# A hybrid retention / gated-attention / mixture-of-experts step on one core: 112 slots per expert block instead of 104, four modulation chunks moved into the second attention's tile loop, three waits moved

## The reference

```
mod = silu(c) @ w_ada + b_ada                       # 6 rows of 1024 for each of 9 conditions
h   = rms_norm(x, norm_pre_mix) * (1 + sc1) + sh1
mix = retention heads (4 x 128) and gated-linear-attention heads (4 x 64 -> 128), then @ w_out
x   = x + g1 * rms_norm(mix, norm_post_mix)
h   = rms_norm(x, norm_pre_ffn) * (1 + sc2) + sh2
f   = shared SwiGLU(h) + sum over 8 of 64 experts of weight * SwiGLU_e(h)   # FF = 256
x   = x + g2 * rms_norm(f, norm_post_ffn)
```

## Time and profile before

| | before |
|---|---|
| median of 3 runs | 1509.92 us (1502.13 to 1510.57) |
| the profiled execution | 1510.28 us |
| its span | 1508.4 us (1.9 us lie around it) |
| PE / DVE / ACT / POOL busy | 1290.0 / 875.9 / 600.8 / 220.2 us |
| moved by DMA | 339.20 MB |

### The profile page before, as it was taken

How to read it: one execution, slowest core, us unless ns; L and a number is a source line. 1 busy time by engine, 2 the same in 40 slices (tenths; PEclk the granted TensorE clock), 3 DMA queues, 4 the chain that set the end, 5 groups by cost and what they waited for, 6 DMA issues and landing times.

```text
span 1508.4 us, 18589 instructions
## 1 busy us (share of the span) xinstructions
PE 1290.0 (86%) x5990; PEld 856.4 (57%) x5990; DVE 875.9 (58%) x1354; ACT 600.8 (40%) x711; POOL 220.2 (15%) x184
## 2 busy tenths in 40 slices
PE   8899999697887896849759999999999999999810
PEld 1599999551455133344446766666666666666500
DVE  0621341243322823246548888888788777788777
ACT  1332221102203001110227767676766666666501
POOL 0100000000000200010012232222222223232211
PEclk9699999897855798959869999999999999999955
DMA  8232221407300591120399999999999999999796
GB/s 330 80 115 91 65 65 33 115 7 237 120 1 4 160 273 50 49 84 1 127 332 357 366 369 365 367 364 365 365 374 357 366 359 355 361 357 372 293 321 223
DMA packets 93567, 339.20 MB, mean 225 GB/s; under 512 B 14360, under 2 KB 37928, under 8 KB 67468
## 3 DMA queue, kind: packets, MB, share of 16 engines
q1 hardware_dynamic: 75104, 301.01, 57.2%
q0 software_dynamic: 18432, 37.79, 7.5%
HBM read 315.13 MB, written 40.39 MB: 236 GB/s over the span
## 4 chain that ended last, share of the span: by engine, by line
PE 52%; DMA 32%; DVE 8%; ACT 3%; issue 3%; SPq 1%; POOL 0%; POOLq 0%; DVEq 0%; ACTq 0%
DMA expert_rows<-arena,row_idx 14%; PE ps L1556 12%; DMA arena<-in_w_exp_down 12%; PE ps L1761 5%; PE ps L1892 4%; PE ps L1587 3%; DMA arena<-expert_rows 2%; PE ps L1797 2%; PE ps L1876 2%; PE ps L1872 2%; PE ps L1504 2%; PE ps L1873 2%; PE ps L1874 2%; DVE down_lo L1398 2%; ACT down_hi L971 2%
## 5 line engine op out<-in xcount | busy, mean ns | idle before, releaser
L1403 DVE TENSOR_TENSOR gu_lo<-w_gu,gu_hi 128x1536 fp32r<-128x1536 f32 x128 | 224.4, 1754 | 2.9 <-ACT gu_hi L965 1.4
L1398 DVE TENSOR_TENSOR down_lo<-arena,down_hi 128x2048 fp32r<-128x2048 f32 x64 | 146.7, 2292 | 85.1 <-ACT down_hi L971 85.1
L965 ACT ACTIVATE gu_hi<-w_gu 128x1536 fp32r<-128x1536 f32 x128 | 189.5, 1481 | 0.1
L1872 PE MATMUL ps<-gu_hi,xT_hi 128*104 128x512 f32 x384 | 157.7, 411 | 12.0 <-issue 7.0
L737 POOL DMA_INDIRECT expert_rows<-arena,row_idx x64 | 104.4, 1631 | 428.2 <-DMA expert_rows<-arena,row_idx 197.2
L1873 PE MATMUL ps<-gu_lo,xT_hi 128*104 128x512 f32 x384 | 153.0, 398 | 0.0
L1874 PE MATMUL ps<-gu_hi,xT_lo 128*104 128x512 f32 x384 | 152.5, 397 | 0.0
L1556 PE MATMUL ps<-w_hi,hT_hi 128*128 128x300 f32 (+1 forms) x480 | 145.8, 304 | 2.3 <-DVE w_lo L1037 2.3
L1556 PE MATMUL ps<-w_lo,hT_hi 128*128 128x300 f32 (+1 forms) x480 | 145.3, 303 | 0.0
L1556 PE MATMUL ps<-w_hi,hT_lo 128*128 128x300 f32 (+1 forms) x480 | 145.1, 302 | 0.0
L971 ACT ACTIVATE down_hi<-arena 128x2048 fp32r<-128x2048 f32 x64 | 122.4, 1912 | 55.4 <-DMA arena<-in_w_exp_down 55.2
(11 more groups left out here) (267 smaller groups left out, 1957.6 us busy)
## 6 DMA issues: line engine op xcount, KB each, us to landing
w_gu<-in_w_exp_gate SPq DMA_DIRECT2D x64, 1024.0 KB
w_gu<-in_w_exp_up SPq DMA_DIRECT2D x64, 1024.0 KB
arena<-in_w_exp_down SPq DMA_DIRECT2D x64, 1024.0 KB
arena<-in_w_ada SPq DMA_DIRECT2D x24, 1024.0 KB, 5.5
arena<-in_w_in SPq DMA_DIRECT2D x12, 1200.0 KB, 5.7
arena<-expert_rows SPq DMA_DIRECT2D x9, 1024.0 KB, 15.9
arena<-expert_rows SPq DMA_DIRECT2D x4, 2048.0 KB, 14.6
arena<-in_x_prompt SPq DMA_DIRECT2D x8, 512.0 KB, 10.5
```

What stands on the lines that cost most here:

```text
L965: a.activation(gu_hi[b % RING][:, :, ks], w_gu[b % U][:, :, ks], ACT.Copy).then_inc(s_ghi, 1)
L1398: v.tensor_tensor(down_lo[:, :, :], w_dn[b % RING], down_hi[:, :, :].bitcast(F32), ALU.subtract).then_inc(s_dlo, 1)
L1403: v.tensor_tensor(gu_lo[b % U][:, :, ks], w_gu[b % U][:, :, ks], gu_hi[b % RING][:, :, ks].bitcast(F32), ALU.subtract).then_inc(s_glo, 1)
L1872: pe.matmul(out, x_hi, gu_hi[r][:, :, k], start=(k == 0), stop=False)
```

## The change

- `T` goes from 104 to 112 (with it the sizes of the slot buffers and the bound `MAX_BLOCKS`, from 108 to 105).
- PE and DVE wait for the states where head 0 first uses them, and not ahead of the retention.
- The store of the prompt state counts on `s_st`. DVE no longer waits for the stores ahead of the gate copies; it waits for the states and the prompt store ahead of the log gates.
- Chunks 0 to 3 of the second modulation leave their two places. `mod_part` issues a quarter of a chunk (two of the eight matmuls; the last with the bias), and tile t of the tile loop, t = 0 to 3, holds the four parts of chunk t; all four use PSUM bank 2. `mod_fold(t - 1)` stands at the head of DVE's tile t.

```
-T = 104
+T = 112
-        MOD2_BANK = (4, 5, 6, 2, 2, 3, 6, 7)
+        MOD2_BANK = (2, 2, 2, 2, 2, 3, 6, 7)
...
-            sp.dma_start(ret_p[0, 0].rearrange("h d v -> d h v"), ret_out).then_inc(s_out, 16)
+            sp.dma_start(ret_p[0, 0].rearrange("h d v -> d h v"), ret_out).then_inc(s_st, 16)
...
@@ vector
-            v.wait_ge(s_st, 16 * (1 + H))
             for h in range(H):
...
                 v.wait_ge(s_rso, h + 1)
+                if h == 0:
+                    v.wait_ge(s_st, 16 * (1 + H))
...
             v.wait_ge(s_rste, 1)
-            v.wait_ge(s_out, 32)
...
+            v.wait_ge(s_st, 16 * (2 + H))
             v.wait_ge(s_l, 2)
...
-            for n in range(3):
-                mod_fold(n)
...
-            mod_fold(3)
             for t in range(NT):
                 R = ROWS[t]
+                if t:
+                    mod_fold(t - 1)
...
@@ tensor
+            def mod_part(n, part):
+
+                i, ks = 2 * n + part // 2, (0, 1) if part % 2 == 0 else (2, 3)
+                if part % 2 == 0:
+                    pe.wait_ge(s_wada[i % 3], 16 * (i // 3 + 3))
+                for k in ks:
+                    o = pe.matmul(ps[0:NCOND, MOD2_BANK[n]], condT[:, 4 * (part // 2) + k, :], w_mod2[i % 3][:, k],
+                                  start=(part == 0 and k == 0), stop=False)
+                if part % 2:
+                    o.then_inc(s_ada, 1)
+                if part == 3:
+                    pe.wait_ge(s_rows, 16 * 6)
+                    pe.matmul(ps[0:NCOND, MOD2_BANK[n]], K("ones", 33)[32:33, 0:NCOND], mod2_bias[:, n], start=False, stop=True).then_inc(s_mod, 1)
...
-            pe.wait_ge(s_st, 16 * (1 + H))
             for h in range(H):
...
                 if h:
                     pe.wait_ge(s_rsoe, h)
+                if h == 0:
+                    pe.wait_ge(s_st, 16 * (1 + H))
...
-            for n in range(3):
-                mod_mm(n)
             pe.wait_ge(s_ls, 2)
...
-                    mod_mm(3)
-                    pe.wait_ge(s_fold, 2 + 3)
...
+                if t < PT:
+                    pe.wait_ge(s_fold, 2 + t)
+                    mod_part(t, 0)
                 pe.wait_ge(s_gte, 2 * t + 2)
...
                         o.then_inc(s_kv, 1)
+                        mod_part(t, 1 + c)
+                    mod_part(t, 3)
                 pe.wait_ge(s_gp, t + 1)
```

More of the change, by code:

```diff
@@ L375, in hybrid_step @@
         s_pj_ev = sem("proj_ready")
-        s_st = sem("states_in")
+        s_st = sem("states_in_and_prompt_state_out")
         s_v = sem("vector_step")
@@ L580, in _ @@
             sp.wait_ge(s_goe, NT)
-            sp.wait_ge(s_out, 16 * (2 + 2 * H))
+            sp.wait_ge(s_out, 16 * (1 + 2 * H))
             sp.dma_start(w_out_buf, w_out[0].rearrange("(k p) n -> p k n", p=P)).then_inc(s_wout, 16)
@@ L685, in _ @@
                 sp.dma_start(tok_rows(y_prompt, y_sample, t), ranks_high[t][0:ROWS[t], 1]).then_inc(s_out, 16)
-            sp.wait_ge(s_out, 16 * (2 + 2 * H + NT))
+            sp.wait_ge(s_out, 16 * (1 + 2 * H + NT))
         @block.gpsimd
@@ L1579, in _ @@
                         project(2 * i + b, b, t)
-            def mod_mm(n):
[L1583 to L1591, removed]
+            def mod_part(n, part):
[10 more added lines that the diff above has]
+                    pe.matmul(ps[0:NCOND, MOD2_BANK[n]], K("ones", 33)[32:33, 0:NCOND], mod2_bias[:, n], start=False, stop=True).then_inc(s_mod, 1)
+            def mod_mm(n):
+                for part in range(4):
+                    mod_part(n, part)
             pe.wait_ge(s_const, 32)
```

## The result

The changed kernel takes 1456.47 us (median of 4 runs, 1451.47 to 1460.36) against 1508.43 us of the kernel before: ratio 0.966, with a 95% interval of 0.9616 to 0.9705. The direction held. The range (1455 to 1494) held by 1.5 us, and only because I had drawn it out to a rival to which I gave 18 in 100; the forecast's own range, 1466 to 1486, did not hold. I forecast 35 us less and it is 52. The two profiled executions are further apart than the medians, 1510.3 to 1451.5 us, of which 4.5 us arose ahead of any edit: the retention's operands are ready at 276.4 us before and at 271.9 after. In the twelve profiles of the changed kernel and its variants, whose code is alike up to there, that point lies between 271.9 and 276.7 us.

What follows compares the result with a forecast made beforehand. Bounds: transfer waits and PE's order before the tile loop, PE at 1.2 GHz in it, serial scatters in the expert blocks. 1510.3 - 8.0 (states) - 9.4 (stores) - 23.4 + 4 + 1.3 + 3 - 2 (chunks) + 0 (slots) = 1475.8, called 1475; range 1455 to 1494.

Steps and rivals of the forecast that it cites:

- a rival to which I gave 18 in 100: Expert blocks: 112 rows shorten the scatter until PE is the bound, 18 us less, result 1458; chance 18 in 100.
- The dealing: Expert blocks' gathers and scatters: each transfer uses the most DMA engines, up to 16, dividing its rows (13 at 104, 16 at 112).

## What to carry over

Where an indirect transfer shares busy DMA engines with other loads, count its packets and try row counts that give fewer of them: 112 or 105 here, not 104 and least of all 108. It is one number, and it was worth 21 us, two thirds as much as the careful edits of the order together. When one row of a profile contradicts a rule, look for the form of the rule that the row fits before setting it aside. Work that is moved into a gap should end just where the next busy stretch begins, since that stretch then starts at the high clock (here that was worth 1.6 us). A shared semaphore that counts loads nobody needs yet is a wait of its own.

## What was unexpected in the hardware

- Packets of an indirect transfer follow the divisors of its rows: 144, 128, 160, 128 with 104, 105, 108, 112 rows. 105 rows cost less than 104, and 108 most.
- The number of slots shows in other transfers: ACT waited 55.2 us for the down weights with 104 slots, 21.3 with 105, 37.9 with 108 and 0 with 112, and the 1 MB reads behind the blocks landed in 15.9 us against 12.6 to 13.1 with 112. The dealing alone does not explain it: with 104 slots and both transfers at 112 rows these are 51.5 and 15.1 us.
- Mixed sizes (gather 104, scatter 112) were no mean of the two: 10.29 us a block, against 10.19 and 9.96 to 10.10, one trace each. This is not explained.
- The page's line on HBM rises by 2.1 MB read and 2.1 MB written from 104 to 112 slots (315.13 to 317.24, 40.39 to 42.48). That is eight rows of 4 KB in 64 blocks, as if padded slots counted, while the queue's bytes stay at 37.8 MB. Why the two differ is open.
- How long TensorE stays at the low clock after the same wait differs from one execution of a kernel to the next, and with it the retention by 3.4 us (55.0 and 58.4).
- TensorE's granted clock in the tile loop went from 0.50 to 1.00 (1.2 to 2.4 GHz) with a chunk's 16 full-height products (and 2 of its bias) put into each tile, and fell back to 0.50 in the 46 us behind it, where PE was busy for 33.3 us with products on 64 rows.
